# Down products of three stages as seven half products instead of eight

## The chip, the cores and the metric

The kernel runs on one core of one Trainium2 chip. The metric is the device time of one execution in microseconds (us), the median of several runs. TensorE (PE in the profile) multiplies 128x128 stationary blocks with up to 512 columns; PEld is its weight load. VectorE (DVE), ScalarE (ACT) and GpSimd (POOL) work element by element, SyncE (SP) issues most DMAs. SBUF is the on-chip memory, a bank is 128x512 float32 of the accumulation memory PSUM.

## Reference

Two layers on 1024 tokens of width 1024: attention and a recurrent group with a SwiGLU network behind it (stage F0), then a gated short convolution mixer (stage S) and a second SwiGLU network (stage F1). The three stages have one form, a wide input product, an elementwise step, and a *down product* that is scaled and added to the stream h:

```python
def swiglu(h, w_gu, w_down):
    gt, up = jnp.split(h @ w_gu, 2, axis=-1)
    return (jax.nn.silu(gt) * up) @ w_down

def short_conv_mixer(h, w_in, w_conv, w_out):
    bg, cg, xv = jnp.split(h @ w_in, 3, axis=-1)
    return (bg * dwconv(cg * xv, w_conv, SC_PAD)) @ w_out

h = h + g1 * y
h = h + g2 * swiglu(modulate(rmsnorm(h, norm2_g[l]), sh2, sc2), ffn_w_gu[l], ffn_w_down[l])
```

The hidden width is 2816 (22 tiles of 128) in F0 and F1 and 1024 (8 tiles) in S. All is float32 in and out.

## The kernel before

**Products.** Every float32 operand is split in two parts, high (ScalarE rounds it) and low (the difference), and a product is three matmuls on 128x512 tiles: high by high, low by high, high by low (lines 1102 to 1104).

**Pairs.** The input product of a stage runs over *pairs* p: two weight columns of 128 (gate and up) against all tokens. There are 22 pairs in F0 and F1 and 12 in S. A pair is done with seven products of half size (Strassen's scheme in Winograd's form, products n = 0 to 6, each 4 x 3 matmuls), so 84 matmuls. The seven weight operands of a pair come out of `pair_raw`, two buffers of 512 KB that SyncE loads (`load_pair`, line 774). VectorE makes sums of them (`weight_sum`, lines 2098 to 2115), ScalarE the high parts (`operand_high`, line 1621), GpSimd the low parts (`operand_low`, line 1063). There is one slot for each n, so the high part n of pair p+1 waits for product n of pair p. `pair_raw` has one generation: the load of buffer 0 of the next pair waits for the low part n = 6, that of buffer 1 for the low part n = 5:

```python
def load_pair(st, p, b):
    if p:
        sp.wait_ge(s_wlo, operand_at(st, (4 if p == 2 else 5) if b else 6, p - 1) + 1)
```

The first four pairs have their products 0 and 3 ahead of all others, so pairs 1 to 3 have five products in the loop and all later ones seven. VectorE combines the products of the pair (`pair_sums`) and makes the hidden tile z in `silu_g` (lines 2275 and 2292) or, in S, in `conv_t`; SyncE stores it to `z_spill` (line 783).

**Down.** `down_products` goes over rounds of two hidden tiles: 16 groups (8 output tiles x 2 token halves) of 2 x 3 matmuls, each group ended by an update of h on VectorE (line 2057); the last two rounds share their groups. Operands come from `z_spill` and the weights in three rotating sets; ScalarE makes the high parts (line 1661), GpSimd the low parts (line 1074). In F0 the 48 `mod_unit` operations on VectorE (line 2070), which make the modulation vectors of the second layer, run between the updates, and `mod_totals` (line 1145) on TensorE sums them. h stays in SBUF.

**End.** The finished rows of 1024 are normalised (`fin_row`, line 2329) and stored.

Of the kernel before, what the change touches and what calls it, by code (L numbers as in the profile page):

```python
# [24 lines left out]
ALU = mybir.AluOpType  # L25
# [5 lines left out]
P = 128  # L31
# [27 lines left out]
def backbone(nc, t):  # L59
# [18 lines left out]
    with es:  # L78
# [19 lines left out]
        z_spill = nc.dram_tensor("z_spill", (HID // P, P, SEQ), F32, kind="Internal").ap()  # L98
# [18 lines left out]
        silu_g = at(88, "silu_g", [P, 2, HALF])  # L117
        mod_in_f = at(80, "mod_in_f", [P, 4, UNIT])
        conv_t = at(88, "conv_t", [P, 2, SEQ])
# [7 lines left out]
        mod_ring = at(0, "mod_ring", [P, 8, UNIT])  # L127
        proj_lo = at(0, "proj_lo", [P, FT, SEQ], F32R)
# [66 lines left out]
        gain_row = at(48, "gain_row", [P, D])  # L195
        fin_rows = [at(kb, f"fin_rows{j}", [P, D]) for j, kb in enumerate((32, 36, 40, 44))]
# [34 lines left out]
        def out_slot(j):  # L231
# [10 lines left out]
        s_par, s_ident, s_turn, s_par_t = sem("par_landed"), sem("ident_made"), sem("x_turned"), sem("par_turned")  # L242
        s_cond, s_param = sem("cond_ready"), sem("par_placed")
        THEN = ("_then_qk_hi_stored0", "_then_qk_hi_stored1", "_then_qk_lo_stored0", "_then_qk_lo_stored1", "_then_qk_lo_stored2",
                "_then_head_landed0", "_then_head_landed1", "", "", "")
        s_x = [sem(f"x_landed{j}{THEN[j]}") for j in range(TT + CT)]
        s_qh, s_ql, s_head, X_DONE = s_x[0:2], s_x[2:5], s_x[5:7], 16
        s_xp, s_xsq, s_xstd, s_xinv = sem("x_placed"), sem("x_squared"), sem("x_rms_ready"), sem("x_inverse_ready")
        s_xm, s_xma = sem("x_modulated_by_dve"), sem("x_modulated_by_act")
        s_mod = [sem(f"mod_landed{j}") for j in range(8)]  # L250
# [28 lines left out]
        s_vst, s_vraw, s_vp = [sem(f"v_stored{j}") for j in range(5)], sem("v_landed"), sem("v_split")  # L279
# [13 lines left out]
        s_zst = (sem("z_stored0"), sem("z_stored1"))  # L293
        s_down = {"a0": sem("set_a_first_half_landed"), "a1": sem("set_a_second_half_landed"), "b": sem("set_b_landed"), "c": sem("set_c_landed")}
        s_h2, s_l2 = sem("down_operand_hi"), sem("down_operand_lo")
        s_n0, s_fs, s_hs, s_ld = sem("first_half_lo"), sem("token_sums_made"), sem("token_operand_hi"), sem("token_operand_lo")
        s_grow = sem("gain_row_landed")
        s_fturn, s_fsq, s_fstd = sem("fin_turned"), sem("fin_squared"), sem("fin_rms_ready")
        s_fta, s_fpart = sem("fin_first_half_turned"), sem("fin_first_half_squared")
        s_fscale, s_fin = sem("fin_scale_ready"), sem("fin_row_ready")  # L300
        s_store = [sem(f"stored{j}") for j in range(4)]
# [7 lines left out]
        FIN_GROUP = (4, 5, 2, 4, 5, 4, 5, 4)  # L309
        FIN_BANK = (6, 6, 0, 6, 2, 0, 6, 4)  # L310
# [91 lines left out]
        ROUND = (HID // (2 * P), FT // 2, HID // (2 * P))  # L402
        PAIR0 = (0, PAIRS[F0], PAIRS[F0] + PAIRS[S])
        OUT = (2 * FT, 2 * FT + 16 * (ROUND[F0] - 1), 2 * FT + 16 * (ROUND[F0] + ROUND[S] - 2))
        NORM = (N_F0, N_S, N_F1)
        LAST_OUT = (0, OUT[F0] + 16 * (ROUND[F0] - 2), OUT[S] + 16 * (ROUND[S] - 2))
        X_BANK = (0, 3, 4, 5)
        BANKS = ({1: 2, 2: 1, 4: 6, 6: 0, 5: 1}, {1: 7, 2: 6, 4: 2, 5: 0, 6: 1}, {1: 7, 2: 1, 4: 6, 5: 2, 6: 1})
        DOWN_BANK = (0, 3, 4, 5)
# [2187 lines left out]
```

## Time and profile before

| | us |
|---|---|
| three runs | 2290.49, 2291.04, 2293.44; median 2291.04 |
| span of the profiled execution, first to last instruction | 2288.6 |
| TensorE busy | 2234.8 (98%) |
| VectorE, GpSimd, ScalarE busy | 1484.0, 1143.8, 840.3 |

No time but the span is known of the profiled execution; it lies 2.4 us below the median of the runs. In the timeline view a row is the start, the duration, the engine, the line, the operation with output and inputs, and in brackets the idle time ahead of it and who ended it. Matmuls overlap: a row's duration is longer than the step from one row to the next.

### The profile page before, as it was taken

To read this page: it belongs to the slowest core of one execution; us is meant where nothing else is said; L and a number is where in the kernel's file an instruction comes from. 1 tells how busy PE (TensorE), PEld (TensorE's weight loads), DVE (VectorE), ACT (ScalarE), POOL (GpSimd) and SP (SyncE) were. 2 spreads that over 40 slices of the span, in tenths; PEclk is the share of its full clock that TensorE was granted. 3 is DMA by queue.
4 is the path that set the end of the run, shared out by engine and by line. 5 is a ranking of instruction groups with operands and counts; after the bars stand their busy time and mean duration, and the time that the engine had idled before them with its cause. 6 is when DMAs were issued, how large, how long until landed. Compare 5 with 4: busy or idle time off the path is not lost.

```text
span 2288.6 us, 27308 instructions
## 1 busy us (share of the span) xinstructions
PE 2234.8 (98%) x10246; PEld 1822.6 (80%) x10246; DVE 1484.0 (65%) x1897; ACT 840.3 (37%) x1396; POOL 1143.8 (50%) x726
## 2 busy tenths in 40 slices
PE   8999999999899999999999999999899999999998
PEld 3788887878688888888888778888688888888886
DVE  5677856854876555558777987665965555555553
ACT  4555546853523332331213522233533333332212
POOL 3323304788455555565434345574365555564340
PEclk9999999999999999999999999999999999999999
DMA  9756568734132222257662122260132222242321
GB/s 332 223 159 175 159 177 205 163 131 134 42 101 83 83 83 83 83 192 258 207 208 78 51 74 74 74 215 2 60 102 90 83 83 83 84 151 90 111 83 74
DMA packets 296942, 282.95 MB, mean 124 GB/s; under 512 B 64783, under 2 KB 242155, under 8 KB 296299
## 3 DMA queue, kind: packets, MB, share of 16 engines
q1 hardware_dynamic: 258747, 257.61, 36.4%
q10 hardware_dynamic: 37488, 21.50, 3.3%
q0 software_dynamic: 576, 2.10, 0.2%
q8 instruction: 82, 1.34, 0.2%
q14 instruction: 49, 0.40, 0.1%
HBM read 226.36 MB, written 57.16 MB: 124 GB/s over the span
## 4 chain that ended last, share of the span: by engine, by line
PE 85%; DVE 6%; DMA 2%; ACT 2%; issue 2%; POOL 1%; SPq 0%; ACTq 0%; DVEq 0%; POOLq 0%
PE bank L1102 27%; PE bank L1104 26%; PE bank L1103 26%; PE bank L1191 1%; DMA q_spill<-qk_raw 1%; PE bank L1332 1%; DVE act_lo L2138 1%; DVE act_hi L2138 1%; PE bank L1357 1%; PE bank L1145 1%; PE bank L1316 1%; PE bank L1358 0%; DVE probs L2519 0%; DVE x_rms L2130 0%; DMA k_lo<-k_spill 0%
## 5 line engine op out<-in xcount | busy, mean ns | idle before, releaser
L2057 DVE SCALAR_TENSOR_TENSOR h<-bank,mods,h 128x512 f32<-128x512 f32 x384 | 287.4, 750 | 260.4 <-PE bank L1104 255.3
L1063 POOL TENSOR_TENSOR slot_lo<-pair_raw,slot_hi 128x512 fp32r<-128x512 f32 x112 | 169.8, 1516 | 288.0 <-ACT slot_hi L1621 288.0
L1063 POOL TENSOR_TENSOR slot_lo<-t_sum,slot_hi 128x512 fp32r<-128x512 f32 x109 | 164.5, 1531 | 153.4 <-ACT slot_hi L1621 153.4
L1063 POOL TENSOR_TENSOR slot<-pair_raw,slot 128x512 fp32r<-128x512 f32 x144 | 232.2, 1634 | 16.0 <-ACT slot L1621 16.0
L2218 DVE TENSOR_TENSOR bank<-bank,p 128x512 f32<-128x512 f32 x53 | 37.0, 698 | 288.3 <-PE bank L1104 288.2
L1102 PE MATMUL bank<-act_lo,slot_hi 128*128 128x512 f32 x436 | 171.1, 392 | 6.6 <-DVE act_lo L2138 5.9
L1621 ACT CAST slot_hi<-pair_raw 128x512 fp32r<-128x512 f32 x112 | 69.0, 616 | 294.4 <-DMA pair_raw<-in_ffn_w_gu 243.6
L1102 PE MATMUL bank<-a,slot_hi 128*128 128x512 f32 x436 | 171.5, 393 | 2.8 <-ACT p L1630 0.9
L1104 PE MATMUL bank<-a,slot_hi 128*128 128x512 f32 x436 | 170.5, 391 | 0.0
L1103 PE MATMUL bank<-act_lo,slot_lo 128*128 128x512 f32 x436 | 169.9, 390 | 0.0
L1104 PE MATMUL bank<-act_lo,slot_hi 128*128 128x512 f32 x436 | 169.9, 390 | 0.0
L1103 PE MATMUL bank<-a,slot_lo 128*128 128x512 f32 x436 | 169.7, 389 | 0.0
L1102 PE MATMUL bank<-act_hi,w_hi 128*128 128x512 f32 x368 | 146.7, 399 | 3.3 <-DVE proj_lo L2392 2.7
L1103 PE MATMUL bank<-act_hi,w_lo 128*128 128x512 f32 x376 | 148.0, 394 | 0.0
L1074 POOL TENSOR_TENSOR act_lo<-low_f,act_lo 128x512 fp32r<-128x512 f32 x80 | 102.3, 1315 | 85.3 <-ACT act_lo L1661 85.3
L1103 PE MATMUL bank<-act_hi,slot 128*128 128x512 f32 x364 | 141.9, 390 | 0.0
L1104 PE MATMUL bank<-act_hi,slot 128*128 128x512 f32 x364 | 141.8, 390 | 0.0
L1102 PE MATMUL bank<-act_hi,slot 128*128 128x512 f32 x364 | 141.7, 389 | 0.0
L1621 ACT CAST slot_hi<-t_sum 128x512 fp32r<-128x512 f32 x109 | 67.8, 622 | 160.6 <-PE bank L1104 103.3
L1102 PE MATMUL bank<-act_lo 128*128 128x512 f32 x320 | 125.8, 393 | 0.0
L1104 PE MATMUL bank<-act_lo 128*128 128x512 f32 x320 | 125.1, 391 | 0.0
L1103 PE MATMUL bank<-act_lo 128*128 128x512 f32 x320 | 124.6, 389 | 0.0
(329 smaller groups left out, 5975.0 us busy)
## 6 DMA issues: line engine op xcount, KB each, us to landing
pair_raw<-in_ffn_w_gu SPq DMA_DIRECT2D x88, 512.0 KB, 4.6
mod_in_f<-in_mod_w SPq DMA_DIRECT2D x48, 512.0 KB, 3.7
z_spill<-silu_g SPq DMA_DIRECT2D x88, 256.0 KB, 2.6
mod_in_p<-in_mod_w SPq DMA_DIRECT2D x32, 512.0 KB, 4.5
pair_raw<-in_o_w_in SPq DMA_DIRECT2D x24, 512.0 KB, 3.8
raw<-in_e_w_in SPq DMA_DIRECT2D x20, 512.0 KB, 4.4
low_f<-z_spill SPq DMA_DIRECT2D x40, 256.0 KB, 5.1
a_f<-z_spill SPq DMA_DIRECT2D x18, 512.0 KB, 6.2
```

The source lines that it names most:

```text
L1063: nc.gpsimd.tensor_tensor(low, from_, high, ALU.subtract).then_inc(s_wlo, 1)
L1074: nc.gpsimd.tensor_tensor(lo, full, hi, ALU.subtract).then_inc(s_l2, 1)
L1102: pe.matmul(dst, w_hi, x_hi, start=first, stop=False)
L1103: pe.matmul(dst, w_lo, x_hi, start=False, stop=False)
L1104: return pe.matmul(dst, w_hi, x_lo, start=False, stop=last)
L1145: mm = pe.matmul(bank[:, b, m:m + 1], acc[:, m * P:(m + 1) * P], ones[:, 0:1], start=True, stop=True)
L1191: mm = pe.matmul(bank[0:2, 4 + 2 * c + a, :], cond[:, k, :], mod_ring[:, u % 8, a * HALF:(a + 1) * HALF], start=(k == 0), stop=(k == FT - 1))
L1316: pe.matmul(out_, q, kh[:, part], start=True, stop=False)
L1621: nc.scalar.copy(slot(st, n, p)[0], from_).then_inc(s_whi, 1)
L2057: V.scalar_tensor_tensor(out=dst, in0=bank[:, b, :], scalar=mods[:, gate, m:m + 1], in1=dst, op0=ALU.mult, op1=ALU.add).then_inc(s_hup, 1)
L2138: V.tensor_tensor(lo, LOW_F[n][k], hi, ALU.subtract).then_inc(s_ld, 1)
L2218: V.tensor_tensor(to, bank[:, x_bank(p), :], p1_at(p), ALU.add).then_inc(s_made, 1)
```

## The change

The down product becomes seven half products too: the hidden tiles are taken two by two (kp, 11 in F0 and F1, 4 in S), the weights of a kp are four blocks of 128x512, and each of the seven products runs over all kp and stays in four banks (`DOWN`). What a product gives goes to the quadrants of h that it belongs to (`UPDATES`); four of the seven carry on in banks that hold an earlier product. The operands are blocks or sums of blocks:

- Sums of z (T1 to T4) are made by VectorE in the pairs (`z_sum`, four for a kp) and stored to `z_parts`.
- Sums of weights (S1 to S4) are made by GpSimd in the pairs (`w_sum`, four for a kp, from pair 4 on, eight in three pairs), between the low parts n = 2, 4, 5 and the next. SyncE loads their blocks to `w_part` a pair ahead, stores the sums to `w_sums`, and issues both behind the next pair's loads (`aside_work`).
- The room for `w_part` is that of h: h is written to HBM in pair 1 and read back in the last pair but one.
- `mod_unit` moves from F0's down product to the pairs of F0 (two in each of pairs 4 to 19) and S (two in each of pairs 2 to 9), and adds up in SBUF, no longer in a bank.
- Down steps have a ring of 8, with the low part of one operand on GpSimd and of the other on VectorE. The end of the kernel works on half rows in part.

```diff
+        B11, B21, B22, T1, T2, T3, T4 = range(7)
+        S1, S3, S2, S4 = range(4)
+        DOWN = (((0, 0), B11, XS, True), (S2, T2, YS, True), ((1, 0), B21, XS, False), (S3, T3, YS, False),
+                ((1, 1), T4, YS, False), (S1, T1, XS, True), (S4, B22, XS, False))
+        UPDATES = (((0, 1), (1, 0), (1, 1)), ((0, 1),), ((0, 0),), ((1, 1),), ((1, 0),), ((1, 1),), ((0, 1),))
+        TAIL = 4
+        BOTH = 4
+        RING = 8
+        W_PAIR = 4
+        def w_ops(st, p):
+            return [k for k in range(4 * KP[st]) if W_PAIR + k // 8 * 3 + k % 8 // 3 == p]
+        def w_loads(st, p):
+            return [kp for kp in range(KP[st]) if W_PAIR + kp // 2 * 3 + kp % 2 - 1 == p]
+        MOD_FROM = (4, 2)
+        MOD_UNITS = (range(0, 4 * FT), range(4 * FT, MODS * FT))
...
+            def aside_work(st, p):
+                for k in w_ops(st, p):
+                    store_w(st, k)
+                for r in w_loads(st, p):
+                    load_w(st, r)
+                for u in mod_units(st, p + 1):
+                    load_mod_f(u)
+                if p == PAIRS[st] - 2:
+                    bring_h_back(st)
...
                 for p in range(1, PAIRS[st]):
+                    z_from = pair_kind(st, p - 1)[0] != "sum"
+                    if z_from:
+                        store_b(st, p - 1, 0)
+                    if p > 1 and p + 1 < PAIRS[st]:
+                        load_pair(st, p + 1, 1)
+                    if z_from and st != S:
+                        store_b(st, p - 1, 1)
+                    if p > 1 and p + 1 < PAIRS[st]:
+                        load_pair(st, p + 1, 0)
...
                     if p == 1:
+                        put_h_aside(st)
...
+                    if st != S and p % 2 == 0:
+                        for c in (T3, T2, T4):
+                            store_t(KP0[st] + p // 2 - 1, c)
+                    aside_work(st, p)
...
+            def w_sum(st, k):
...
+                if c == S1:
+                    pool.wait_ge(s_wld[kp % 2], 64 * (kp // 2 + 1))
+                    ins = nc.gpsimd.tensor_tensor(a22_, a21_, a22_, ALU.add)
+                elif c == S3:
+                    ins = nc.gpsimd.tensor_tensor(a21_, a11_, a21_, ALU.subtract)
...
                 for p in range(1, PAIRS[st]):
+                    sums = w_ops(st, p)
                     for n in operands(st, p):
                         operand_low(st, n, p)
+                        if n in (2, 4, 5) and len(sums) > n // 2 - (n < 5):
+                            w_sum(st, sums[n // 2 - (n < 5)])
...
+            def before_pair(st, p):
...
+                if st != S and p % 2:
+                    dve.wait_ge(s_z1, PAIR0[st] + p)
+                    z_sum(KP0[st] + p // 2, T1)
+                if st != S and p % 2 == 0 and p:
+                    for c in (T2, T4):
+                        z_sum(KP0[st] + p // 2 - 1, c)
+                for u in mod_units(st, p):
                     mod_unit(u)
...
+            def down_products(st):
+                n = steps_of(st)
+                for i in range(n - TAIL):
+                    down_ready(st, i)
+                    for m in range(4):
+                        mm = down_part(st, i, m)
...
```

## Rows read from the trace of the kernel before

**Rows 1.** The page: span; engine, busy us (share of the span) x instructions.

```profile
span 2288.6 us, 27308 instructions
PE 2234.8 (98%) x10246; PEld 1822.6 (80%) x10246; DVE 1484.0 (65%) x1897; ACT 840.3 (37%) x1396; POOL 1143.8 (50%) x726
```

**Rows 2.** Windows: stretch, busy us (instructions) of each engine, PEclk, DMA share, GB/s.

```profile
650.00:1010.00 360.00, 360.00 (x1584) 296.94 (x1583) 203.87 (x249) 111.90 (x192) 205.78 (x134) 1.00 0.28 87
1014.00:1260.00 246.00, 246.00 (x1139) 205.06 (x1138) 185.40 (x239) 62.95 (x92) 117.70 (x69) 1.00 0.59 200
2036.00:2240.00 204.00, 204.00 (x900) 168.66 (x899) 109.58 (x146) 40.40 (x52) 99.95 (x55) 1.00 0.29 101
```

**Rows 3.** Page, costliest groups: updates of h; busy, mean ns, idle before, its releaser.

```profile
L2057 DVE SCALAR_TENSOR_TENSOR h<-bank,mods,h 128x512 f32<-128x512 f32 x384 | 287.4, 750 | 260.4 <-PE bank L1104 255.3
```

**Rows 4.** Timeline of SyncE in F0's first pairs: stores of z, loads of buffer 0.

```profile
633.44 7.87 SPq L783 DMA_DIRECT2D z_spill<-silu_g  x3
...
646.04 0.38 SPq L774 DMA_DIRECT2D pair_raw<-in_ffn_w_gu  x1
...
660.39 0.38 SPq L774 DMA_DIRECT2D pair_raw<-in_ffn_w_gu  x1
...
677.51 0.38 SPq L774 DMA_DIRECT2D pair_raw<-in_ffn_w_gu  x1
...
694.57 0.38 SPq L774 DMA_DIRECT2D pair_raw<-in_ffn_w_gu  x1
...
731.32 0.38 SPq L774 DMA_DIRECT2D pair_raw<-in_ffn_w_gu  x1
...
750.49 0.38 SPq L774 DMA_DIRECT2D pair_raw<-in_ffn_w_gu  x1
```

**Rows 5.** Timeline of GpSimd: first, second and last low parts of pair 5.

```profile
683.45 1.30 POOL L1063 TENSOR_TENSOR slot_lo<-pair_raw,slot_hi 128x512 fp32r<-128x512 f32 x1 [5.97 <-ACT slot_hi L1621]
684.70 3.01 POOL L1063 TENSOR_TENSOR slot_lo<-t_sum,slot_hi 128x512 fp32r<-128x512 f32 x2
...
692.80 1.75 POOL L1063 TENSOR_TENSOR slot<-pair_raw,slot 128x512 fp32r<-128x512 f32 x1
```

**Rows 6.** Timeline of ScalarE: the first high part of pair 5.

```profile
682.75 0.62 ACT L1621 CAST slot_hi<-pair_raw 128x512 fp32r<-128x512 f32 x1 [6.94 <-DMA pair_raw<-in_ffn_w_gu]
```

**Rows 7.** Timeline: the first low part of pair 4, and TensorE's product with it.

```profile
666.38 1.30 POOL L1063 TENSOR_TENSOR slot_lo<-pair_raw,slot_hi 128x512 fp32r<-128x512 f32 x1 [6.02 <-ACT slot_hi L1621]
668.97 0.39 PE L1102 MATMUL bank<-a,slot_hi 128*128 128x512 f32 x1
```

**Rows 8.** Timeline of VectorE: two operations with both inputs in SBUF.

```profile
842.97 1.79 DVE L2292 TENSOR_TENSOR silu_g<-silu_g,t_pad 128x512 f32<-128x512 f32 x1
...
854.07 0.68 DVE L2098 TENSOR_TENSOR t_sum<-pair_raw 128x512 f32<-128x512 f32 x1
```

**Rows 9.** Single lines over the whole run: count, min/median/max ns, first and last start.

```profile
L1063 POOL TENSOR_TENSOR slot<-pair_raw,slot x144: 1294/1751/1839, 609.3 to 2016.1; 128x512 fp32r<-128x512 f32 x144
L1063 POOL TENSOR_TENSOR slot_lo<-t_sum,slot_hi x109: 1282/1306/1848, 593.0 to 2009.7; 128x512 fp32r<-128x512 f32 x109
L2449 DVE SCALAR_TENSOR_TENSOR mod_acc_p<-mod_in_p,cond,mod_acc_p x28: 1276/1285/3419, 121.4 to 329.6; 128x1024 f32<-128x1024 f32 x28
L2329 DVE SCALAR_TENSOR_TENSOR fin_rows<-bank,fin_scale,gain_row x8: 1283/1284/1285, 2257.1 to 2284.2; 128x1024 f32<-128x1024 f32 x8
```

**Rows 10.** DMA issues: tensor, engine, count, KB each, median us from issue to landing.

```profile
pair_raw<-in_ffn_w_gu SPq DMA_DIRECT2D x88, 512.0 KB, 4.6
...
h_spill<-h_in ACTq DMA_DIRECT2D x1, 4096.0 KB, 13.7
...
low_c<-in_ffn_w_down SPq DMA_DIRECT2D x12, 512.0 KB, 7.3
```

**Rows 11.** Timeline of TensorE in S: the first product of pair 4.

```profile
1356.40 0.47 PE L1102 MATMUL bank<-a,slot_hi 128*128 128x512 f32 x1 [0.77 <-POOL slot_lo L1063]
```

More of the change, by code:

```diff
@@ new lines, in down_landed, with down_high_at, down_low_at @@
+        def down_landed(st, i):
+            before = sum((steps_of(k) - i % RING + RING - 1) // RING for k in range(st))
+            return s_land[i % RING], MOD_DONE + 32 * (before + i // RING + 1)
+        def down_high_at(st, i, j):
+            return s_h2, 2 * sum(steps_of(k) for k in range(st)) + 2 * i + j + 1
+        def down_low_at(st, i, j):
+            if j == 1 and i >= BOTH:
+                return s_lz, sum(steps_of(k) - BOTH for k in range(st)) + i - BOTH + 1
+            return s_l2, sum(steps_of(k) + BOTH for k in range(st)) + (2 * i + j + 1 if i < BOTH else i + BOTH + 1)
@@ new lines, in down_part @@
+            def down_part(st, i, m):
+                q, r = divmod(i, KP[st])
+                banks, fresh = DOWN[q][2:]
+                if r == 0:
+                    bank_free(st, q, m)
+                w, x = down_operand(i)
+                at_ = slice(m * P, (m + 1) * P)
+                end = r == KP[st] - 1
+                mm = product(bank[:, banks[m], :], (w[0][:, at_], w[1][:, at_]), x[0], x[1], fresh and r == 0, end, not fresh)
+                if end:
+                    mm.then_inc(s_out, 1)
+                return mm
@@ L2263, in pair_work @@
                 kind, tile = pair_kind(st, p)
-                first, x = p1_at(p), bank[:, x_bank(p), :] if p else silu_g[:, 0, :]
+                first, x = p1_at(p), bank[:, x_bank(p), :] if p else zt[:, 0, one]
+                z_one, z_two = zt[:, p % 2, one], zt[:, p % 2, two]
                 ahead = p + 1 if p + 1 < PAIRS[st] else None
                 gated = sum((PAIRS[F0], PAIRS[S] // 3)[:st]) + (p // 3 if st == S else p)
+                before_pair(st, p)
                 if p:
@@ L2306, in mods_here @@
-            def mods_here(r, idx):
-                for u in mod_units(r, idx):
+                        steps.run(V.scalar_tensor_tensor(out=zt[:, tile % 2, :], in0=t_pad[:, j:j + SEQ], scalar=par[:, c:c + 1],
+                                                         in1=zt[:, tile % 2, :], op0=ALU.mult, op1=ALU.add))
+                else:
+                    V.tensor_tensor(zt[:, 0, two], first, zt[:, 0, two], ALU.mult).then_inc(s_z0, 1)
+                    V.tensor_tensor(zt[:, 1, two], c22, zt[:, 1, two], ALU.mult).then_inc(s_z1, 1)
```

928 lines of the change are left out of this document (538 added, 390 removed).

## Prediction

> **What bounds the kernel now.** I read the page's first part first: TensorE is busy for 98% of the span, and no other engine comes near [rows 1]. So every matmul taken away is worth its step, unless its place is taken by a wait. The windows give the step: 1584 matmuls in 360.0 us of the pairs of F0, and 900 in 204.0 us of the down product of F1, are both 0.227 us for one, at a granted clock of 1.00 [rows 2]. The duration of a single row (0.39 us) overlaps with the next and must not be used. The updates of h wait for TensorE (255 of their 260 us of idle time), so the VectorE work of the down product is covered [rows 3].
>
> The second question is how far TensorE's lead reaches in the pairs, since the change puts work there. A pair has 84 matmuls: 84 x 0.227 = 19.1 us. Against that stands a closed chain. The load of `pair_raw` buffer 0 waits for the last low part of the pair before it, and that pair's low parts wait for their own load. I read it link by link for pair 5: the load is issued at 677.51 [rows 4]; ScalarE, which waited for that DMA, begins at 682.75 [rows 6]; GpSimd, idle for 5.97 us, makes the first low part at 683.45 and, without a break, the others until 694.55 [rows 5]; the next load goes out at 694.57 [rows 4]. In this stretch the chain runs at its own pace: the load of pair 4 at 660.39, of pair 5 at 677.51, of pair 6 at 694.57, 17.1 us each. Later the loads stand 19.2 us apart (731.32 to 750.49): by then the chain is ahead and TensorE sets the pace. So the chain has 2.0 us of slack in a pair, no more, although GpSimd is busy for only 205.8 of 360 us [rows 2]. Its idle time lies in the chain, as the wait for a DMA that it has itself released.
>
> One more reading gives the price of an operation in the chain. Pair 3 has five low parts, and its load and the next are 14.35 us apart (646.04 to 660.39); pairs 4 and 5 have seven and 17.1: (17.1 - 14.35) / 2 = 1.4 us for one [rows 4]. The operation alone takes 1.29 to 1.3 us (the minimum), and 1.75 in the median of one form [rows 9]. The excess is VectorE: an operation of VectorE with both inputs in SBUF takes 0.68 us when GpSimd stands still (line 2098) and 1.79 us when it is at work (line 2292) [rows 8]. The two take turns, and each turn of VectorE makes GpSimd later.
>
> **What it saves.** The down product of F0 and of F1 had 11 rounds x 16 groups x 6 = 1056 matmuls each, that of S 4 x 16 x 6 = 384. Seven half products over 11 kp have 7 x 11 x 4 x 3 = 924, over 4 kp 336. So 132 + 132 + 48 = 312 matmuls go, and 312 x 0.227 = 70.9 us. TensorE had no idle time there, so all of it counts if the new steps keep it fed. A step is 12 matmuls, 2.73 us, with 512 KB of operands: 192 GB/s. F0's down product moved 200 GB/s at a DMA share of 0.59 with TensorE busy for 246 of 246 us [rows 2], so I take it as fed. GpSimd (1.3 us) and VectorE (0.68) make one low part each in a step and fit. The updates fall from 384 - 16 = 368 to 108, all beside TensorE.
>
> **What the sums cost in the pairs.** GpSimd's weight sums stand in the chain: behind n = 2, 4, 5, that is ahead of the last low part, which releases the load. Eight in three pairs at 1.3 us are 3.5 us for a pair, 1.5 more than the slack of 2.0. This is the step on which the forecast rests. Queued behind them are the low parts n = 3 to 6 of the next pair, and for these wait VectorE's last weight sum, SyncE's two loads and TensorE.
>
> VectorE gets two z sums a pair in F0 and F1 (four in three pairs in S), at 0.68 us, both inputs in SBUF. They begin behind its last multiplication, about when GpSimd ends its chain. Bounds: 0 (all in GpSimd's wait for the DMA) and 1.4 us a pair; I take half, 0.7, and 0.5 in S. The `mod_unit` operations take 1.28 us alone (3.4 at most where GpSimd worked beside them [rows 9]); two a pair follow the z sums, deeper in that wait. Bounds: 0 and 2.6 us; I take 0.5, nearer the lower end, since 6 us of wait are there. Their cover is that wait; VectorE itself (203.9 of 360 us busy) has room.
>
> - F1: 17.1 + 3.5 + 0.7 = 21.3 us a pair against 19.1, so 2.2 us for each of 17 pairs (sums in the chains of pairs 4 to 20, so pairs 5 to 21 are late) = 37. The chain's lead at pair 4 comes off: its first low part ends at 667.68, TensorE takes it at 668.97, 1.3 us [rows 7]. 36 us.
> - F0: the same, and 0.5 in 16 pairs: 44 us.
> - S: 17.1 + 3.5 + 0.5 + 0.5 = 21.6, so 2.5 us for 6 pairs = 15. No lead comes off: TensorE already waits 0.77 us for that low part at pair 4 [rows 11].
>
> Together 95 us.
>
> The Trainium skill ("SBUF — State Buffer", section "Who interferes with whom") says that a VectorE instruction with two SBUF inputs and a GpSimd one that reads SBUF exclude each other for the whole instruction. The rows above agree on the exclusion (1.79 against 0.68). Strictly applied, each z sum and `mod_unit` would count in full; that is the third rival.
>
> **Smaller terms.** SyncE's queue gets stores, loads of weight blocks, and `mod_unit` loads, all behind the next pair's loads; they hold those up only if SyncE or the DMA engines are not through in the 13 us until the next; taken as 0, the other end is the second rival. Writing h (4 MB) in pair 1 stands ahead of the loads of pair 3; such a write took 13.7 us [rows 10], and it stands behind the stores of pair 0 (the first at 633.44), 12.6 us ahead of the load of buffer 0 at 646.04 [rows 4]; that load and the one of buffer 1 before it find the queue full, and I take a slip of 3 us a stage (0 to 6): 9 us. Reading h back lies before no pair load: 0. Where a product carries on in the banks of the one just before it, the update (0.75 us [rows 3]) must come in the 2.0 us until the bank's turn; a low part ahead of it can spoil that: 1 us a stage (0 to 3): 3 us. At the end, four of eight 1.28 us row operations [rows 9] become half as long: -2 us (-4 to 0). `mod_totals` moves at its old price: 0.
>
> **Sum.** The profiled span, 2288.6 us, is 2.4 below the median, so I set the changes on the median: 2291.0 - 70.9 + 95 + 9 + 3 - 2 = **2325 us**. With everything but GpSimd's own 1.3 us at its lower end: 24 + 24 + 9 = 57 for the pairs, 2291 - 71 + 57 - 4 = 2273. With the z sums in full, half of the `mod_unit`s and all small terms at their upper end: 48 + 69 + 22 = 139, and 28: 2387; I cut this range at 2380, since all ends at once are unlikely.
>
> **Rivals.**
>
> 1. *The weight sums ride in GpSimd's idle time and TensorE keeps the pace.* For it: 8.2 of 19.1 us of a pair are idle on GpSimd [rows 2], the sums need 3.5, and `operand_low` has slack for several pairs late in a stage. Against it: the chain's own pace of 17.1 us, seen where TensorE did not set it. It would hold if a weight sum cost the chain under 0.75 us (2.0 / 2.67); and even above that the kernel is faster as long as the pairs lose less than 1.6 us each (40 pairs, 64 us, against 71 + 2 saved and 9 + 3 of small terms, with 2.6 of lead). Time: 2291 - 71 + 10 - 2 = 2228 us, or up to 2273 where it holds in part.
> 2. *The transfers collide.* A pair moved 87 GB/s in F0 [rows 2], 1.7 MB; with sums, blocks and `mod_unit` loads it is over 3 MB, and loads of 512 KB in company took 7.3 us to land instead of 4.6 [rows 10]. 2 us more in 40 chains are 80 us: 2405 us. The same end would be reached if the down steps starved.
> 3. *The turns of VectorE count in full.* 48 + 90 + 30 = 168 us for the pairs: 2398 us.
>
> **How the numbers follow.** The forecast has a chance of 0.60, rival 1 0.24, rival 2 0.10, rival 3 0.06. A measurement of this kernel tells 0.2% (4.6 us) from no change. The forecast's own range is 2273 to 2380; since both signs are possible, the range that should hold 8 in 10 takes in rival 1: 2222 to 2380, which leaves out rivals 2 and 3 and small tails. Faster: 0.24 and 0.08 of the forecast's lower end, 0.32; same 0.03; slower 0.65.
>
> **What the profile after would show.** Right: in pairs 6 to 20 of F1 the loads of `pair_raw` buffer 0 are 21 us apart, TensorE has about 2 us of idle time a pair, released by GpSimd's `slot_lo`, GpSimd works without a break but for 6 us, and the down products take 210 us in F0 and F1 (77 x 2.73) and 76 in S with TensorE full. Wrong: loads 19.1 us apart (rival 1); ScalarE's wait for the DMA well over 7 us (rival 2); chains of 23 us and more in F0 against 21 in F1 (rival 3); gaps of TensorE in the down steps (the saving is mis-sized). If a weight sum on GpSimd takes clearly less than 1.3 us, the forecast falls.

## The result, and the profile after

The changed kernel takes **2361.2 us** (median of 2359.6 to 2363.6) against 2292.2 of the kernel before in the same comparison: 1.030 times as long (95% interval 1.029 to 1.032), +69 us. The forecast was 2325 us, slower by 34. The sign and the range held, and in F0 and F1 the mechanism did too; the loss is twice the forecast, and the second half of it lies in stage S, where other waits than those of the forecast made it.

The page of the changed kernel, part one (answers to [rows 1]):

```profile
span 2357.6 us, 27816 instructions
PE 2203.5 (93%) x9934; PEld 1774.6 (75%) x9934; DVE 1768.2 (75%) x1915; ACT 938.5 (40%) x1620; POOL 1353.2 (57%) x880
```

TensorE has less to do and is busy for 93%, not 98%. The windows, cut at the first matmul of each stage, tell where (columns as in [rows 2]; the order is F0 pairs, F0 down, S pairs, S down, F1 pairs, F1 down):

```profile
583.70:1057.20 473.50, 444.94 (x1929) 358.28 (x1928) 416.80 (x414) 142.21 (x247) 305.39 (x196) 0.99 0.56 195
1057.20:1272.20 215.00, 212.72 (x941) 174.93 (x941) 147.70 (x141) 108.09 (x191) 137.01 (x94) 1.00 0.62 199
1272.20:1556.80 284.60, 250.29 (x1057) 199.86 (x1057) 243.55 (x262) 81.28 (x133) 158.87 (x99) 0.95 0.46 158
1556.80:1658.70 101.90, 82.95 (x354) 66.66 (x352) 75.27 (x90) 46.73 (x85) 56.32 (x39) 0.94 0.54 175
1658.70:2129.40 470.70, 436.59 (x1864) 349.96 (x1865) 373.17 (x382) 145.09 (x252) 301.55 (x196) 0.99 0.47 160
2129.40:2346.00 216.60, 216.21 (x976) 178.63 (x976) 131.07 (x126) 95.88 (x176) 114.16 (x79) 1.00 0.60 196
```

Of the kernel before, the same two windows of S:

```profile
1265.80:1511.40 245.60, 236.92 (x1025) 191.00 (x1024) 193.29 (x231) 82.04 (x135) 122.51 (x82) 0.99 0.26 80
1511.40:1601.00 89.60, 89.60 (x401) 73.86 (x400) 53.92 (x77) 34.35 (x55) 53.28 (x35) 1.00 0.32 95
```

Its other stages were 431.1 (F0 pairs), 253.0 (F0 down), 431.1 (F1 pairs) and 244.6 us (F1 down). Against the terms of the forecast (`mod_totals` apart: one takes TensorE 1.70 us in the trace of before, 1090.91 to 1092.61; four are now in F0's pairs and two in S's, all six were in F0's down product):

| stage | change, us | of it `mod_totals` | rest | forecast |
|---|---|---|---|---|
| F0 pairs | +42.4 | +6.8 | +35.6 | 44 + 3 |
| F1 pairs | +39.6 | 0 | +39.6 | 36 + 3 |
| F0 down | -38.0 | -10.2 | -27.8 | -30 + 1 |
| F1 down | -28.0 | 0 | -28.0 | -30 + 1 |
| **S pairs** | +39.0 | +3.4 | **+35.6** | 15 + 3 |
| **S down** | +12.3 | 0 | **+12.3** | -11 + 1 |
| start and end | +1.8 | 0 | +1.8 | -2 |

F1 is near the forecast, F0's pairs are 11 us better than it; S is 40 us worse (17.6 in the pairs, 22.3 in the down product).

**The chain in F1.** Answering to [rows 4], SyncE's loads of the pairs (buffer 1 first; an x2 row holds both buffers):

```profile
1783.88 3.35 SPq L830 DMA_DIRECT2D pair_raw<-in_ffn_w_gu  x2
...
1804.46 0.38 SPq L830 DMA_DIRECT2D pair_raw<-in_ffn_w_gu  x1
...
1806.17 0.38 SPq L830 DMA_DIRECT2D pair_raw<-in_ffn_w_gu  x1
...
1825.65 3.35 SPq L830 DMA_DIRECT2D pair_raw<-in_ffn_w_gu  x2
...
1846.26 0.38 SPq L830 DMA_DIRECT2D pair_raw<-in_ffn_w_gu  x1
```

From the first load of a pair to that of the next (1783.88 to 1846.26) these are three steps in 62.4 us, 20.8 each, and 20.9 on average up to 2055.93; the forecast was 21.3. GpSimd in one pair (answers to [rows 5]; L1153 is a low part, L1171 and L1174 are weight sums):

```profile
1792.11 1.30 POOL L1153 TENSOR_TENSOR slot_lo<-pair_raw,slot_hi 128x512 fp32r<-128x512 f32 x1 [5.28 <-ACT slot_hi L1753]
1793.36 2.97 POOL L1153 TENSOR_TENSOR slot_lo<-t_sum,slot_hi 128x512 fp32r<-128x512 f32 x2
1796.29 1.75 POOL L1171 TENSOR_TENSOR w_part<-w_part 128x512 f32<-128x512 f32 x1
...
1800.98 1.74 POOL L1174 TENSOR_TENSOR w_part<-w_part 128x512 f32<-128x512 f32 x1
1802.67 3.48 POOL L1153 TENSOR_TENSOR slot<-pair_raw,slot 128x512 fp32r<-128x512 f32 x2
```

It works without a break from 1792.11 to 1806.15, the load of buffer 0 goes out at 1806.17, and then GpSimd stands for 6.80 us, as it stood in the kernel before. ScalarE beside it (L1753 is a high part, L1771 the SiLU of the pair before):

```profile
1792.43 0.62 ACT L1753 CAST slot_hi<-t_sum 128x512 fp32r<-128x512 f32 x1 [0.40 <-DVE t_sum L2288]
1794.04 0.62 ACT L1753 CAST slot_hi<-t_sum 128x512 fp32r<-128x512 f32 x1 [0.99 <-DVE t_sum L2295]
1794.56 0.59 ACT L1771 ACTIVATE zt<-bank 128x512 f32<-128x512 f32 x1
```

The waits of TensorE, first in the pairs of F1 from 1760 on, then in those of S (the columns: who waited for whom, us in total, times, the longest):

```profile
PE bank L1230 <- ACT zt L1771: 24.8, 15, 3.3
```

```profile
PE bank L1230 <- DVE p L2408: 16.1, 5, 8.2
PE bank L1230 <- DVE t_pad L2466: 9.8, 3, 4.5
...
PE bank L1230 <- DVE zt L2468: 1.2, 1, 1.2
```

In F1 that is 1.65 us for each of 15 pairs. In S the waits are of another kind: VectorE ends them. All waits of S's pairs together are 34.3 us; in the kernel before they are 8.7.

**One gap of S**, the longest of its pairs. SyncE, VectorE and TensorE at the start of the fourth pair:

```profile
1354.25 2.10 SPq L830 DMA_DIRECT2D pair_raw<-in_o_w_in  x2
1356.40 2.98 SPq L833 DMA_DIRECT2D z_parts<-zt  x4
```

```profile
1357.87 0.69 DVE L2509 TENSOR_TENSOR p<-zt 128x512 f32<-128x512 f32 x1
1363.22 0.69 DVE L2513 TENSOR_TENSOR zt<-zt,p 128x512 f32<-128x512 f32 x1 [4.67 <-DMA z_parts<-zt]
1363.83 3.67 DVE L2260 SCALAR_TENSOR_TENSOR mod_acc_f<-mod_in_f,cond,mod_acc_f 128x1024 f32<-128x1024 f32 x2
1367.42 0.69 DVE L2404 TENSOR_TENSOR bank<-bank,p 128x512 f32<-128x512 f32 x1
1368.02 0.68 DVE L2408 TENSOR_TENSOR p<-bank,p 128x512 f32<-128x512 f32 x1
```

```profile
1368.76 0.80 PE L1230 MATMUL bank<-a,slot 128*128 128x512 f32 x1 [8.19 <-DVE p L2408]
...
1369.78 0.63 PE L1232 MATMUL bank<-a,slot 128*128 128x512 f32 x1
1370.20 0.63 PE L1230 MATMUL bank<-a,slot 128*128 128x512 f32 x1
...
1373.91 0.39 PE L1230 MATMUL bank<-a,slot_hi 128*128 128x512 f32 x1
```

T4 (L2513) overwrites block B21, so it waits until B21 is stored; SyncE issues that store behind the loads of the next pair. Behind T4 stand the two `mod_unit` operations, and behind these the sums that free TensorE's bank. The windows of these microseconds show a second price:

```profile
1356.00:1360.00 4.00, 4.00 (x19) 3.25 (x18) 2.49 (x4) 0.00 (x0) 0.00 (x0) 1.00 0.84 228
1364.00:1368.00 4.00, 0.00 (x0) 0.00 (x0) 3.90 (x3) 0.00 (x0) 1.03 (x1) 0.50 0.79 225
1368.00:1372.00 4.00, 3.25 (x8) 2.58 (x9) 3.83 (x7) 1.43 (x3) 1.19 (x1) 0.50 0.94 347
1372.00:1376.00 4.00, 4.00 (x16) 3.20 (x15) 3.93 (x6) 1.48 (x3) 4.00 (x4) 0.78 0.10 37
```

The granted clock is 0.50 (the lower level, 1.2 GHz) behind the gap, and a matmul's step is 0.42 us (1369.78 to 1370.20), not 0.227. In the timeline of S 54 steps of the changed kernel are of that kind, 6 of the kernel before; at 0.2 us too much for each this is about 10 us. F0's pairs have 29 such steps and F1's 24, where the kernel before has none.

### The profile page after: what moved, and what is told of

It reads as the page before. It is cut to its first block and busy times, and to the rows that moved or that the text cites. A ratio compares the mean times of both kernels' runs of the same rounds, so it can differ in the third digit from the quotient of the medians.

```text
span 2357.6 us, 27816 instructions
## 1 busy us (share of the span) xinstructions
PE 2203.5 (93%) x9934; PEld 1774.6 (75%) x9934; DVE 1768.2 (75%) x1915; ACT 938.5 (40%) x1620; POOL 1353.2 (57%) x880
## 5 line engine op out<-in xcount | busy, mean ns | idle before, releaser
L1153 POOL TENSOR_TENSOR slot_lo<-pair_raw,slot_hi 128x512 fp32r<-128x512 f32 x112 | 172.2, 1537 | 284.4 <-ACT slot_hi L1753 284.4
L1153 POOL TENSOR_TENSOR slot<-pair_raw,slot 128x512 fp32r<-128x512 f32 x144 | 238.0, 1659 | 10.7 <-ACT slot L1753 10.7
L1230 PE MATMUL bank<-a,slot_hi 128*128 128x512 f32 x436 | 181.2, 416 | 62.4 <-ACT zt L1771 42.6
L1753 ACT CAST slot_hi<-pair_raw 128x512 fp32r<-128x512 f32 x112 | 69.1, 617 | 416.0 <-DMA pair_raw<-in_ffn_w_gu 329.4
L1181 POOL TENSOR_TENSOR act_lo<-low_f,act_lo 128x512 fp32r<-128x512 f32 x108 | 154.7, 1444 | 120.7 <-ACT act_lo L1795 120.6
L1153 POOL TENSOR_TENSOR slot_lo<-t_sum,slot_hi 128x512 fp32r<-128x512 f32 x109 | 161.6, 1502 | 96.0 <-ACT slot_hi L1753 96.0
L1231 PE MATMUL bank<-a,slot_lo 128*128 128x512 f32 x436 | 176.1, 404 | 0.0
L1232 PE MATMUL bank<-a,slot_hi 128*128 128x512 f32 x436 | 176.1, 404 | 0.0
L1795 ACT CAST act_lo<-low_f 128x512 fp32r<-128x512 f32 x192 | 109.6, 621 | 142.6 <-DMA low_f<-z_parts 142.6
L1230 PE MATMUL bank<-act_lo 128*128 128x512 f32 x384 | 152.5, 397 | 14.5 <-DVE h L2246 10.5
L1230 PEld LDWEIGHTS bank<-a,slot_hi 128*128 128x128 f32 x436 | 85.0, 195 | 96.5 <-ACT zt L1771 54.2
L1232 PE MATMUL bank<-act_lo 128*128 128x512 f32 x384 | 150.9, 393 | 0.0
L1231 PE MATMUL bank<-act_lo 128*128 128x512 f32 x384 | 150.8, 393 | 0.0
L1753 ACT CAST slot<-pair_raw 128x512 fp32r<-128x512 f32 x144 | 85.7, 620 | 158.7 <-DVE pair_raw L2305 83.4
```

The lines of the kernel that those rows point to most:

```text
L1153: nc.gpsimd.tensor_tensor(low, from_, high, ALU.subtract).then_inc(s_wlo, 1)
L1181: nc.gpsimd.tensor_tensor(lo, full, hi, ALU.subtract).then_inc(s_l2, 1)
L1230: pe.matmul(dst, w_hi, x_hi, start=first, stop=False, skip_group_check=resumed)
L1231: pe.matmul(dst, w_lo, x_hi, start=False, stop=False, skip_group_check=resumed)
L1232: return pe.matmul(dst, w_hi, x_lo, start=False, stop=last, skip_group_check=resumed)
L1753: nc.scalar.copy(slot(st, n, p)[0], from_).then_inc(s_whi, 1)
```

## The experiments

Each row of the table is one kernel: its time (one execution, or the median where an interval is given further down) and the length of the stages, from first matmul to first matmul (F1 down: to its last matmul), in its profiled execution. For e10 and e11 that execution took 2263.1 and 2263.4 us, above their medians.

| kernel | us | F0 pairs | F0 down | S pairs | S down | F1 pairs | F1 down |
|---|---|---|---|---|---|---|---|
| before | 2292.2 | 431.1 | 253.0 | 245.6 | 89.6 | 431.1 | 244.6 |
| changed | 2361.2 | 473.5 | 215.0 | 284.6 | 101.9 | 470.7 | 216.6 |
| e1 sums last | 2280.8 | 444.0 | 214.0 | 266.4 | 103.1 | 437.8 | 215.7 |
| e2 sums thin | 2278.3 | 443.9 | 214.0 | 267.0 | 102.9 | 437.7 | 215.7 |
| e3 T4 later | 2348.8 | 472.8 | 215.2 | 269.3 | 102.7 | 473.5 | 217.3 |
| e4 lows later | 2356.4 | 473.1 | 214.5 | 284.5 | 101.7 | 468.8 | 217.0 |
| e5 four orders | 2270.0 | 444.6 | 214.0 | 256.3 | 96.0 | 445.3 | 215.7 |
| e6 e5, `mod_unit` inside | 2291.5 | 444.9 | 215.6 | 278.6 | 95.7 | 443.9 | 215.7 |
| e7 `mod_unit` thin | 2339.5 | 465.2 | 215.3 | 275.2 | 101.7 | 468.8 | 217.0 |
| e8 z sums thin | 2348.9 | 468.6 | 215.8 | 281.6 | 102.4 | 465.2 | 216.6 |
| e9 loads early | 2357.7 | 474.2 | 215.2 | 284.9 | 98.5 | 468.7 | 216.7 |
| e12 e9, squares thin | 2354.8 | 474.1 | 216.6 | 283.2 | 92.8 | 473.4 | 217.3 |
| e10 best | 2258.0 | 443.2 | 215.6 | 258.2 | 94.1 | 437.7 | 215.7 |
| e11 lows first | 2260.5 | 445.1 | 214.0 | 256.3 | 94.7 | 435.9 | 215.7 |

Stages that an edit does not touch tell how far single executions scatter: F1's pairs take 468.7 to 473.5 us in the changed kernel, e3, e4, e7, e9 and e12, F0's pairs 472.8 to 474.2 in those but e7, and S's pairs 283.2 to 284.9 in the changed kernel, e4, e9 and e12.

### Is it the place of the weight sums, or their work?

**e1.** The sums of a pair behind the last low part, which releases the load, so in GpSimd's own wait for that load.

```diff
                     for n in operands(st, p):
                         operand_low(st, n, p)
-                        if n in (2, 4, 5) and len(sums) > n // 2 - (n < 5):
-                            w_sum(st, sums[n // 2 - (n < 5)])
+                    for k in sums:
+                        w_sum(st, k)
```

> Same work as the changed kernel (2361 us), only GpSimd's order differs: the weight sums of a pair come behind its last low part (n = 6) instead of between the low parts. Theory 1 (the sums cost time because they stand in the closed chain that releases the next load of pair_raw): the chain goes back to 17.1 us plus the z sums, TensorE sets the pace again, loads of buffer 0 in F1 stand 19.1 to 19.7 us apart instead of 20.8; pairs of F1 431 to 442 us instead of 470.7, of F0 433 to 450 instead of 473.5, S 5 to 10 us shorter; total 2275 to 2300. Rival A (it is GpSimd's whole load, with VectorE's turns, wherever the sums stand) and rival B (the added DMA traffic): pairs of F0 and F1 within 8 us of the changed kernel, total 2345 to 2365.

Measured: 2280.8 us, **80 us less** by one edit of order. F1's pairs 437.8 us, F0's 444.0, S's 266.4 (18 us shorter, where I expected 5 to 10). SyncE's loads in F1:

```profile
1902.44 0.38 SPq L830 DMA_DIRECT2D pair_raw<-in_ffn_w_gu  x1
...
1921.64 2.11 SPq L830 DMA_DIRECT2D pair_raw<-in_ffn_w_gu  x2
...
1940.74 0.38 SPq L830 DMA_DIRECT2D pair_raw<-in_ffn_w_gu  x1
...
1959.46 2.09 SPq L830 DMA_DIRECT2D pair_raw<-in_ffn_w_gu  x2
```

19.0 us apart (57.02 in three steps), TensorE's pace, and from 1715 on its trace has no wait of TensorE in F1's pairs. The sums still take 1.73 to 1.74 us in the median (in F1 1.49 to 1.62 in the mean of a form, about 7 us less for its 44 sums, not 33), the DMA share of F1's pairs is 0.51 where it was 0.47: neither GpSimd's load nor the traffic made the loss, the place in the chain did. Rivals A and B fall.

**e2.** The counter-check: the sums stay where they are, on one column.

```diff
-                a11_, a12_, a21_, a22_ = (w_part[:, kp % 2, j, :] for j in range(4))
+                a11_, a12_, a21_, a22_ = (w_part[:, kp % 2, j, 0:1] for j in range(4))
```

> Left out: the weight sums on GpSimd are made on one column of 512 only, so nearly all of their work is missing; all loads, stores and waits stay. Theory 1 (their time in the chain): F1 pairs 431 to 440 us instead of 470.7, F0 433 to 448 instead of 473.5, S 6 to 15 shorter; total 2260 to 2295. Rival B (the traffic of DMA, or SyncE's longer queue, slows the pairs): F0 and F1 pairs at most 8 us shorter, total over 2340. What stays in F0 above 431 is the price of the z sums, the mod_unit operations and the writing of h.

Measured: 2278.3 us, stage for stage within 0.6 us of e1 (S's pairs 18 us shorter than in the changed kernel, 6 to 15 expected). So sums behind the last low part cost nothing that can be seen, and ahead of it they cost 33 us in F1, 30 in F0 and 18 in S. The forecast had 36, 44 and 15 for them together with the sums of z and, in F0 and S, `mod_unit`.

### What VectorE's additions cost

**e8** (z sums) and **e7** (`mod_unit`), both on the changed kernel.

```diff
-                a, b, c_, d, t2 = zt[:, 0, one], zt[:, 0, two], zt[:, 1, one], zt[:, 1, two], p1[:, 1, :]
+                a, b, c_, d, t2 = zt[:, 0, 0:1], zt[:, 0, HALF:HALF + 1], zt[:, 1, 0:1], zt[:, 1, HALF:HALF + 1], p1[:, 1, 0:1]
```

> The changed kernel; left out: the sums of z on VectorE are made on one column of 512 only; their waits, stores and places stay. My prediction priced the two of a pair at 0.7 us in F0 and F1: then the pairs of F1 get 10 to 13 us shorter (470.7 to about 459), those of F0 as much, and S 3 to 6. If they ride in GpSimd's wait for the load: under 4 us in F0 and F1. If VectorE's turns count in full (rival 3): 24 us and more each.

Measured: F1 5.5 us shorter, F0 4.9, S 3.0. Over 17 pairs of F1 that is 0.32 us a pair; the forecast had 0.7, the ends 0 and 1.4. This is between what two theories gave, nearer to "they ride in GpSimd's wait". By the scatter above F1's 5.5 us may be 3.5 to 8.3 (0.2 to 0.5 us a pair), and S's 3.0 us lie little above it.

```diff
+                    w = UNIT if k == FT - 1 else 1
-                    ins = V.scalar_tensor_tensor(out=to[:], in0=from_, scalar=scalar, in1=mod_acc_f[:], op0=ALU.mult, op1=ALU.add)
+                    ins = V.scalar_tensor_tensor(out=to[:, 0:w], in0=from_[:, 0:w], scalar=scalar, in1=mod_acc_f[:, 0:w], op0=ALU.mult, op1=ALU.add)
```

> The changed kernel; left out: six of eight mod_unit operations are made on one column of 1024 only, so three quarters of their work is missing. My prediction priced them at 0.5 us a pair in 16 pairs of F0 and 8 of S: then F0's pairs get 5 to 8 us shorter (473.5 to about 467) and those of S 3 to 4. If they stand ahead of the sums that TensorE waits for in S: S pairs 10 to 20 us shorter (284.6 to 265 to 275). If VectorE's turns count in full (rival 3): F0 20 to 30 us shorter.

Measured: F0 8.3 us shorter for three quarters of the work, so about 11 for all (forecast 8). S 9.4 us shorter, just under the 10 to 20 of the second theory; for all of it about 12.5, where the forecast had 0.5 us in 6 pairs, 3: in S these operations stand ahead of the sums that TensorE waits for.

### What it is in the pairs of S

**e3.** T4 one pair later, with its store and the wait of ScalarE that goes with it (not shown here); nothing else.

```diff
-                    for c in (T1, T3, T2, T4):
+                    for c in (T1, T3, T2):
                         z_sum(KP0[S] + p // 3 - 1, c)
+                if st == S and p % 3 == 1 and p > 1:
+                    z_sum(KP0[S] + p // 3 - 1, T4)
...
```

> Same work as the changed kernel, but in stage S VectorE makes the sum T4 of a hidden pair one pair later, and SyncE stores it one pair later; so VectorE does not wait 4.7 to 5 us for the store of block B21, which SyncE issues behind the next pair's loads. Theory S1 (these waits make TensorE wait 8.2, 2.7 and 3.8 us, and the granted clock falls behind the longest): these three gaps shrink to under 2 us each, the pairs of S take 265 to 273 us instead of 284.6, all else stays, total 2341 to 2350. Rival S2 (VectorE is overloaded in S anyway, the wait only moves): S pairs 279 to 285, total 2355 to 2361.

Measured: S's pairs 269.3 us, 15.3 shorter, in the middle of what theory S1 gave. The gap of 8.2 us is 1.8. Not all went as said: two gaps ahead of another product, released by `t_pad`, are 4.7 and 4.6 us (4.5 at most in the changed kernel).

**e6.** On top of e5 (below), `mod_unit` in S behind the sums of the pair, ahead of z:

```diff
                 else:
                     first_pair_sums(st)
+                if st == S:
+                    mods_here(st, p)
...
```

> As the run with the four orders together, and in S VectorE makes the two mod_unit operations of a pair behind the pair's sums instead of ahead of them, so that they no longer stand ahead of the sums that free TensorE's banks. If what is left in S is that place: S pairs 2 to 8 us shorter than in the run with the four orders, all else equal. Rival (VectorE's total work in S is what counts, 92 of 109 us busy): within 2 us, or longer, since the operations now stand ahead of z and of the next pair's last weight sum.

Measured: 2291.5 us (ratio to before 0.9997, 0.999 to 1.001), S's pairs 278.6 us, **22 us longer** than in e5. My reading of their place was half right: ahead of the sums they cost some 12 us; behind them they stand ahead of z and of the next pair's last weight sum, as the rival said, and cost more. VectorE has hardly an empty place in a pair of S: it is busy for 243.6 of 284.6 us in the changed kernel (rows above) and for 233.8 of 256.3 in e5. Of the 22 us some 10 are the clock: e6 has 51 steps of 0.42 us in S's pairs, e5 none.

### What it is in the down product of S

The changed kernel's longest gap, 8.61 us, stands ahead of product 4, which carries on in the banks of product 3 and waits for its updates. TensorE's waits in S down:

```profile
PE bank L1230 <- DVE h L2246: 14.1, 2, 8.6
PE bank L1230 <- POOL act_lo L1181: 3.1, 1, 3.1
PE bank L1230 <- POOL a L1181: 1.6, 1, 1.6
```

VectorE ahead of the longest, and GpSimd beside it (L2542 is a low part, L2215 a sum of squares for the next norm, L2246 the updates; L1181 is a low part on GpSimd):

```profile
1610.28 1.75 DVE L2542 TENSOR_TENSOR act_lo<-low_f,act_lo 128x512 fp32r<-128x512 f32 x1
1611.95 1.75 DVE L2215 TENSOR_TENSOR sumsq<-sumsq,sq 128x512 f32<-128x512 f32 x1
1613.63 1.75 DVE L2542 TENSOR_TENSOR act_lo<-low_f,act_lo 128x512 fp32r<-128x512 f32 x1
1614.80 1.71 POOL L1181 TENSOR_TENSOR act_lo<-low_f,act_lo 128x512 fp32r<-128x512 f32 x1
1615.30 2.71 DVE L2246 SCALAR_TENSOR_TENSOR h<-bank,mods,h 128x512 f32<-128x512 f32 x4
```

Operations with both inputs in SBUF take 1.75 us, in turns with GpSimd; the updates, with one input in a bank, take 0.68 (four in 2.71) in the same microseconds. That is the rule of the Trainium skill ("SBUF — State Buffer", section "Who interferes with whom"): two SBUF inputs exclude a reading GpSimd, one does not. The rows agree with both halves of it.

**e4.** GpSimd's seven first low parts of the next stage in steps 16 to 22, not 8 to 14.

```diff
-                if k + 4 <= j < k + 11:
-                    operand_low(nx, *FIRST[j - k - 4])
+                at_ = k + 4 if st == F0 else 4 * k
+                if at_ <= j < at_ + 7:
+                    operand_low(nx, *FIRST[j - at_])
```

> Same work as the changed kernel, but in the down product of S GpSimd makes the seven first low parts of the next stage in steps 16 to 22 instead of 8 to 14, so VectorE's low parts and sums of squares in product 3 meet fewer GpSimd operations. Theory D1 (VectorE comes late with the updates of product 3 because its operations take 1.5 to 1.8 us beside GpSimd's instead of 0.7, and product 4 waits 8.6 us for the same banks): that gap falls under 3 us, S's down product takes 88 to 95 us instead of 101.9. Rival D2 (updates, low parts and sums of squares are too many for a product of 10.9 us whatever GpSimd does): gap 6 to 9 us, down product 99 to 103 us, total within 3 us of 2361.

Measured: the gap is 4.4 us, between what the two gave, but one of 3.1 appears later (ahead of the norm), and S down takes 101.7, as D2 said: inconclusive.

**e9.** The trace of the changed kernel has a long wait on an engine that I had not suspected. ScalarE, in order:

```profile
1593.15 0.62 ACT L1753 CAST slot_hi<-slot_lo_f 128x512 fp32r<-128x512 f32 x1 [10.75 <-DMA slot_f<-in_ffn_w_gu]
1593.68 1.14 ACT L1795 CAST act_hi<-x_rms 128x512 fp32r<-128x512 f32 x2
```

It waits for the last of the next stage's first loads, and the high parts of the down steps stand behind. The edit issues these loads early:

```diff
-                    if st != F1 and 10 <= i < 17:
+                    if st == F0 and 10 <= i < 17:
                         load_first(st + 1, i - 10)
+                    if st == S and 7 <= i < 11:
+                        for e in range(2 * i - 14, min(2 * i - 12, 7)):
+                            load_first(st + 1, e)
```

> The changed kernel, only in the down product of S SyncE issues the seven first weight loads of the next stage two by two with the loads of steps 7 to 10 instead of one by one with those of steps 10 to 16. Theory D3 (ScalarE, in order, stands 10 to 11 us at the first high part of the next stage until the last of these loads has landed; the high parts of the down steps behind it come late, then the low parts of VectorE and GpSimd in one crowd, and with them the updates that product 4 waits for): ScalarE's stand goes, the gap of 8.6 us ahead of product 4 falls under 2.5 us, S down 90 to 95 us instead of 101.9, all else within 2 us; total 2349 to 2355. Rival D2 (VectorE has too much to do in a product of 10.9 us): gap 6 to 9 us, S down 99 to 103.

Measured: ScalarE's wait is gone, the gap 4.1 us instead of 8.6, S down 98.5: D3 is right in kind, but it is about half of the gap and 3.4 of the 22 us by which S down was worse than forecast. **e12** adds to it three sums of squares on one column:

```diff
-                w = NORMS[n][2]
+                w = 1 if n == N_F1 and 0 < i < 4 else NORMS[n][2]
```

> The run with the seven first loads early (S down 98.5 us, 4.1 us of gap ahead of product 4), and left out: three of the sums of squares that VectorE makes in product 3 are made on one column of 512 only. If what is left of that gap is VectorE's crowd in product 3 (four low parts and four sums of squares at 1.7 us in turns with GpSimd, and four updates, 16 us against 10.9 for the product): the gap falls under 1 us, S down 93 to 96. Rival (the low parts come late for another reason, from ScalarE or a load): gap 3 to 5 us, S down 97 to 99.

Measured: the gap is 1.6 us (under 1 was expected) and S down 92.8, 5.7 us shorter than in e9: the crowd is most of the rest. Of these 5.7 us 2.5 are the gap and about 2 the clock (18 steps of 0.42 us in e9, 7 in e12). The two longest rows of TensorE's waits in S down, e9 and then e12:

```profile
PE bank L1233 <- DVE h L2249: 9.6, 2, 5.5
PE bank L1233 <- POOL act_lo L1184: 3.6, 1, 3.6
```

```profile
PE bank L1233 <- DVE h L2249: 7.1, 2, 5.5
PE bank L1233 <- POOL act_lo L1184: 3.0, 1, 3.0
```

So two causes made the gap: ScalarE's wait, which pushed the low parts together, and VectorE's crowd in a product of only 10.9 us; 1.6 us of it stay open. The 5.5 us in both are the last updates, which stand behind VectorE's scalings for the next stage. The 3.1 and 1.6 us that GpSimd's low parts end come early in the stage; ahead of the 3.1 ScalarE, which GpSimd's low parts wait for, stood 5.00 and 2.59 us for loads out of `z_parts` (until 1572.63 and 1576.36). No run tried them.

### Put together

**e5** joins e1, e3, an order in which GpSimd's first low parts of the next stage come in every second step and the squares in product 4, and the last updates between the scalings.

> Same work as the changed kernel with four orders changed together: weight sums behind the last low part (2280.8 us alone), T4 a pair later in S, and in the down product of S GpSimd's seven first low parts of the next stage in every second step, the squares of the first half and their sums in product 4 instead of 3, and the updates of the last product between the scalings of the next stage instead of behind them. If the gaps of S are what is left of the miss: S pairs 250 to 258 us (266.4 with the first edit alone), S down 86 to 94 (103.1), pairs of F1 433 to 437 (437.8) since the clock no longer falls ahead of them; total 2248 to 2262. Rival (VectorE is the bound in S, whatever the order): S pairs over 262, S down over 98, total 2270 to 2281.

Measured: 2270.0 us, 0.991 (0.989 to 0.992) of before; slower than I gave. S's pairs came as expected (256.3), S down did not (96.0), and F1's pairs got longer (445.3), since the gap ahead of F1 had only moved: the norm of the second half now waits 7.8 us. **e10** takes the loads of e9 for the move of the squares, and lets VectorE scale one feature ahead, so that it no longer waits for ScalarE's square of the same feature:

```diff
+                if st == S and j == 6 * k - 1:
+                    dve.wait_ge(*updated(st, 3, 3))
+                    scale(n, 2, 2)
+                    down_update(st, 5, 0, *UPDATES[5][0])
+                    scale(n, 3, 3)
+                    for m in (1, 2, 3):
+                        down_update(st, 5, m, *UPDATES[5][0])
+                    for i in range(4):
+                        scale(n, 4 + i, 4 + i)
+                        add_squares(n + 1, i)
+                        down_update(st, 6, i, *UPDATES[6][0])
+                    return
...
```

> Same work as the changed kernel, all orders that helped together: weight sums behind the last low part; T4 a pair later in S; in the down product of S the next stage's first loads early and GpSimd's seven first low parts in every second step; at its end the scalings of the next stage one ahead of the sums of squares that wait for ScalarE, with the updates of the last two products between them. Against the run with the four orders (2270.0 us): S down 86 to 92 us instead of 96, F1's pairs 436 to 442 instead of 445.3; total 2255 to 2263. Rival: the end of S is a chain over ScalarE (three operations for a feature) that no order shortens: total 2267 to 2272.

Measured: **2258.0 us, 0.985 (0.982 to 0.987) of the kernel before**, faster by 34 us where the change as given was slower by 69. F1's pairs are as expected (437.7), S down is not (94.1, with 4.4 us of gap ahead of product 4); the 5.5 us of wait ahead of F1 are gone. **e11** moves GpSimd's seven first low parts ahead of product 3 (steps 7 to 13):

> As the best run so far (2258.0 us), but GpSimd makes its seven first low parts of the next stage in steps 7 to 13 of S's down product, ahead of product 3's crowd, instead of in every second step from 8 to 20. If GpSimd's turns are what makes VectorE's operations of product 3 long: gap ahead of product 4 from 4.4 to under 2.5 us, S down 89 to 92 us instead of 94.1, total 2253 to 2257. Rival (VectorE's operations take turns with GpSimd's low parts of the down steps all the same): S down 93 to 96, total 2257 to 2262.

Measured: 2260.5 us (0.986, 0.984 to 0.988), S down 94.7, the gap 4.45 as in e10: this is what the rival gave, that VectorE's turns are with the low parts of the down steps themselves.

## Why the prediction was right and where it was wrong

- **The saving.** Right: 30 us in each of F0 and F1 forecast, 27.8 and 28.0 found; the down steps are fed (TensorE busy for 212.7 of 215.0 and 216.2 of 216.6 us). In S the 48 matmuls went as well, but 19.0 us without a matmul came in their place (101.9 - 82.95).
- **The closed chain.** Right, and shown by e1 and e2 from both sides. Of its terms, the z sums were 0.32 us a pair, not 0.7. The weight sums have the price that was forecast: with the chain's own 17.1 us as read in F0 of before, 20.9 - 17.1 - 0.3 leaves 3.5 us for a pair, eight thirds of 1.3, although the row of one shows 1.75. The likely reason, argued and not tried, is that VectorE has no more turns to take than before, so that what a turn adds to a weight sum it no longer adds to a low part.
- **What would show it.** The rhythm and the size of the gap were right, the last link wrong: I said that GpSimd's `slot_lo` releases TensorE, and it is ScalarE's SiLU (L1771). It reads the bank that TensorE needs next, and stands on ScalarE behind the high parts of the next pair, which wait for VectorE's sums of the loaded weights (the three rows above). The chain has a branch over ScalarE that is later than the one over GpSimd. The price is the same, and both branches go with e1.
- **Rival 1** (the sums ride in idle time) fell for the kernel as given, and became true with e1: the idle time is there, but behind the last low part. **Rival 2** fell: the traffic is the same in e1. **Rival 3** fell as a sum: the turns are real (1.75 us), but two z sums of a pair (1.36 us alone) cost 0.32.
- **h aside.** Three us a stage forecast; e1 has gaps of 1.1, 0.7 and 0.8 us in the first pairs of F1 that the kernel before has not, 2.5 us. Whether h or the z sums make them was not tried.
- **Where luck came in.** F0's pairs cost 35.6 us where 47 were forecast, though its terms, measured one at a time (30 for the weight sums, 11 for `mod_unit`, 5 for the z sums), make 46. They hide each other in part, and the forecast had added them up; that took 11 us off the miss. Of the -2 us at the end -0.2 came; the other +2.0 of that row is the unchanged part ahead of F0's pairs, which begin at 582.4 to 588.2 us in the runs.
- **S pairs: the first step that failed** (18 us forecast, 35.6 found). I took the chain of F0 and set it into S, and SyncE's added stores and loads at 0. S differs in two ways that the trace of before could have told. Its VectorE was busy for 193.3 of 245.6 us (79%), not 204 of 360, so "VectorE itself has room" was never true there. And the sums of z wait for a store that SyncE issues behind the next pair's loads: I had listed what stands *behind* SyncE's additions, not who waits *for* them. The terms measured one at a time: weight sums 18 us (e1), T4's wait 15 (e3), `mod_unit` about 12 (e7), z sums 3 (e8); together 48, more than the 35.6 found, so they hide each other in part; e1 and e3 in one kernel (e5) give 28.3, alone 18.2 and 15.3. In the trace the 35.6 us are 25.6 more of waits (34.3 against 8.7), and most of the rest is the clock (41 steps of 0.42 us against 6).
- **S down: the second** (10 us less forecast, 12.3 more found). "1 us a stage (0 to 3)" for products that carry on in the banks of the one before. I sized it by one update, 0.75 us, and by the one low part ahead of it. In F0 and F1 a product lasts 11 steps, 30 us, and the term holds (one gap of 1.8 us in F0). In S it lasts 4 steps, 10.9 us, and all that VectorE, ScalarE and GpSimd do for the next stage falls into so few products: 16 us of VectorE's work in product 3 alone. e9 and e12 show two causes of the 8.6 us, and 5.5 us are the end of the stage, which e10's order took away. The other 4.7 us, early in the stage, stay open.
- **A price that I did not have.** Most of the long gaps of S are followed by matmuls at the lower clock, about 10 us in all. I counted a wait as its length.

## What to carry to other kernels

When work is added to an engine that is part of a closed chain (a load that waits for the last reader of its buffer), its place can decide, and not its amount: the same operations cost 33 us in F1 ahead of the instruction that releases the load, and nothing that could be seen behind it, in the wait that the chain has itself. A price worked out for one stage holds for another only if its slack is read there again: the busy share of every engine, the length of a step, and for each added store who waits for it. And an engine in order that does two streams (ScalarE's high parts for this stage and the next) can stall the near one when the far one's load is late, here by 10.75 us.

## What the runs showed of the hardware

The granted clock: TensorE stood for 8.2 us from 1360.6 on; the clock was 0.50 (1.2 GHz) in the windows from 1364 on, still 0.50 in that from 1372 to 1373, and 1.00 in that from 1374 to 1375, five us after the first matmul at 1368.76. The twelve matmuls up to 1373.91 took 5.15 us, where twelve steps of 0.227 are 2.72: 2.4 us more for a gap of 8.2. The turns of VectorE and GpSimd are even: in the rows of S down each of the two starts one operation every 1.67 us (VectorE at 1610.28, 1611.95 and 1613.63), 1.71 to 1.75 us long, where alone it takes 0.68 and 1.30, and operations of VectorE with an input in a bank are not touched (0.68).
